# Nine feature-major tiles of a three-layer transformer computed as 512- and 256-column products in two PSUM banks each

## The chip, the cores and the metric

The kernel runs on one core of a Trainium2 chip. The metric is the time of one execution on the device in microseconds, the median over several runs. The core has TensorE (matrix products into PSUM, eight banks of 512 columns), VectorE, ScalarE and GpSimd (elementwise work), and SyncE, which issues the weight loads. Each has its own instruction stream, and they meet at semaphores only.

## The reference

Three layers work on 256 tokens of width 1024. The first two (a sparse-attention layer and a latent-attention layer, each with an MLP) are untouched here. The third is a hybrid layer:

```python
proj = h @ w_in            # q_m, k_m, v_m, gates, o, q_a, k_a, v_a, gate_pre
...
y_a = (jax.nn.sigmoid(o_pre.astype(f32)) * hm).astype(x.dtype)      # mLSTM branch
...
y_b = jnp.sum(wts[..., None] * jnp.stack(outs, axis=0), axis=0)     # dilated attention on q_a, k_a, v_a
...
g_a, g_b = jnp.split(jax.nn.sigmoid(gate_pre), 2, axis=-1)
merged = g_a * (y_a @ w_proj_a) + g_b * (y_b @ w_proj_b)
x = x + merged @ w_out
hf = rmsnorm(x, norm_ffn_g)
x = x + (jax.nn.silu(hf @ w_gate) * (hf @ w_up)) @ w_down
```

All is float32. `k_a` has 1536 columns, six tiles of 256; `y_a @ w_proj_a` has 1024, four tiles.

## The kernel before, in words

Every float32 weight and activation is kept as two parts, a high part rounded to the type that TensorE takes and the low remainder. A product W x is the sum of three: high x high, high x low, low x high (`three`, L628 to L630).

The weights come in chunks of 1 MB (2048 values in each of 128 partitions). Each goes through the same steps. SyncE loads it into one of two landing buffers (`raw`) once the chunk that was there has its low part. ScalarE copies it to `whi`, rounded (the **split**, `split_one`, L1769), once TensorE is through with the chunk that used this one of three split buffers. VectorE subtracts (`low_part`, L2417) and so makes `wlo`, the **low part**, and that frees the landing buffer; for a few chunks GpSimd does this (L1726). TensorE then uses the chunk. The order of each engine's work is written out by hand: `ahead(name)` and `split_to` on ScalarE, `low_ahead(name)` and `low_to` on VectorE say which chunks are prepared before a given step.

`feature_major(name, x, b)` makes one tile of 256 output features by 256 tokens. For each half of 128 features it adds up eight slices of the contraction, three products of 256 columns each, and both halves lie in one PSUM bank `b`. `open_bank` waits until the bank's last user has been read (`read`), `close_bank` signals `full`.

Around the change the third layer's TensorE program runs thus. Four mLSTM heads, each with one query tile qa0 to qa3 between its products; five key tiles ka1 to ka5 in banks 4 + (j + 2) % 4; four banks of transposes (`C.hT`); the value tiles va; the logits of the dilated attention; eight gate tiles g0 to g7 with the attention's products between them; the four projection tiles pa0 to pa3 in banks 2 and 3 by turns; pb0 and pb1 (`y_b @ w_proj_b`) in banks 4 to 7; then the output product co0 to co3, of which each waits for a tile `C.m{k}.lo` of the merged activations; then the FFN.

VectorE evacuates the tiles. `attention_copy` (L2982) multiplies a key tile by the norm's row scale (L2991); the loop at L3116 multiplies a projection tile by its gate (L3120); the loop at L3122 multiplies pb by its gate (L3128) and adds pa (L3129), and `merged_low` (L2590) makes the low part of each merged tile after ScalarE has made its high part. In the key stage VectorE also normalises the mLSTM's output, `hidden_normed` (L3027) and `hidden_gated` (L3030), between the key tiles. GpSimd has nothing to do in the third layer before the FFN.

The MLPs of the first two layers already have a form of 512- and 256-column products in their up step:

```python
for nt, k in tiles or ((nt, k) for nt in range(2) for k in range(KT)):
    nc.tensor.matmul(psum[:, 4 + 2 * j2 + nt, :], hi[:, k, nt * P:nt * P + P], xA[:, :, k, :],
                     start=k == 0, stop=False)
for nt in range(2):
    for k in range(KT):
        ins = nc.tensor.matmul(psum[:, 4 + 2 * j2 + nt, 0:SEQ], lo[:, k, nt * P:nt * P + P],
                               xA[:, 0, k, :], start=False, stop=k == KT - 1)
```

These are L842 and L846 of the profile: one product of the high weights with both parts of the activations side by side (512 columns), and one of the low weights with the high part (256 columns).

## Time and profile before

| | |
|---|---|
| median of 3 runs | 1105.75 us (1105.38 to 1105.99) |
| the profiled execution's own time | 1105.73 us |
| its span, first to last instruction | 1103.6 us |
| TensorE matmul / VectorE / ScalarE / GpSimd busy | 1090.9 / 757.8 / 600.3 / 149.6 us |
| mean granted TensorE clock | 0.999 of full |
| DMA | 194.00 MB, 176 GB/s in the mean |

The span leaves out 2.1 us at the two ends of the execution. Busy time is the union of an engine's records. TensorE's records overlap, since its products are pipelined: what a product costs is the distance from its start to the next start, not its recorded length.

### The profile page before, as it was taken

How to read it: one execution, taken by the hardware profiler on the slowest of the kernel's cores; microseconds unless marked ns; L12 is line 12 of the kernel's file. 1: busy time of each engine (PE TensorE's matmuls, PEld its weight loads, DVE VectorE, ACT ScalarE, POOL GpSimd, SP SyncE). 2: the span in 40 equal slices, each digit the busy share in tenths (PEclk: the TensorE clock that was granted, in tenths of full speed). 3: DMA queues.
4: the chain of work that ended last, by engine and by line, in shares of the span. 5: the costliest groups of instructions: out<-in, count | busy, mean ns of one | idle time of the engine just before them, and what ended most of it. 6: DMA issues, size and time to landing. Idle time of an engine off the chain costs nothing.

```text
span 1103.6 us, 17798 instructions
## 1 busy us (share of the span) xinstructions
PE 1090.9 (99%) x6977; PEld 973.0 (88%) x6977; DVE 757.8 (69%) x1054; ACT 600.3 (54%) x788; POOL 149.6 (14%) x113
## 2 busy tenths in 40 slices
PE   8999999999999999999999999999999999999997
PEld 7868888888998888888889999898899989999997
DVE  6774665656668466656557878576587577988884
ACT  6574644444698464444455546555555357546454
POOL 4652000000377220000030000000000002000003
PEclk9999999999999999999999999999999999999999
DMA  9836565556433156565645654446653556545631
GB/s 303 289 117 123 188 223 191 191 190 233 138 106 129 33 161 217 187 195 189 200 154 191 191 158 144 131 153 231 201 166 121 168 214 229 200 176 196 226 136 39
DMA packets 138929, 194.00 MB, mean 176 GB/s; under 512 B 7163, under 2 KB 113112, under 8 KB 138860
## 3 DMA queue, kind: packets, MB, share of 16 engines
q1 hardware_dynamic: 129004, 184.02, 50.7%
q10 hardware_dynamic: 9248, 8.95, 3.2%
q8 instruction: 47, 0.77, 0.3%
q0 software_dynamic: 608, 0.08, 0.1%
q14 instruction: 22, 0.18, 0.0%
HBM read 191.90 MB, written 6.37 MB: 180 GB/s over the span
## 4 chain that ended last, share of the span: by engine, by line
PE 91%; ACT 4%; DVE 4%; issue 1%; DVEq 0%; ACTq 0%
PE psum L628 22%; PE psum L629 22%; PE psum L630 22%; PE psum L842 11%; PE psum L846 6%; ACT arena L1755 3%; PE psum L716 2%; PE psum L746 1%; PE psum L1392 1%; PE psum L1419 1%; DVE arena L2711 1%; DVE st L2710 1%; PE psum L1353 0%; PE psum L904 0%; PE psum L906 0%
## 5 line engine op out<-in xcount | busy, mean ns | idle before, releaser
L2417 DVE TENSOR_TENSOR wlo<-raw,whi 128x2048 fp32r<-128x2048 f32 (+1 forms) x134 | 302.4, 2264 | 134.8 <-ACT whi L1769 133.7
L1769 ACT ACTIVATE whi<-raw 128x2048 fp32r<-128x2048 f32 (+1 forms) x149 | 277.4, 1871 | 174.0 <-PE psum L630 126.3
L628 PE MATMUL psum<-xA,whi 128*128 128x256 f32 x840 | 239.2, 285 | 0.0
L630 PE MATMUL psum<-xA,wlo 128*128 128x256 f32 x840 | 237.6, 283 | 0.0
L629 PE MATMUL psum<-xA,whi 128*128 128x256 f32 x840 | 237.6, 283 | 0.0
L1726 POOL TENSOR_TENSOR wlo<-raw,whi 128x288 fp32r<-128x288 f32 (+3 forms) x43 | 81.8, 1930 | 746.5 <-ACT whi L1769 746.2
L628 PEld LDWEIGHTS psum<-xA,whi 128*128 128x128 f32 x840 | 160.3, 191 | 2.9 <-DVE wlo L2648 0.9
L629 PEld LDWEIGHTS psum<-xA,whi 128*128 128x128 f32 x840 | 160.4, 191 | 1.1
L630 PEld LDWEIGHTS psum<-xA,wlo 128*128 128x128 f32 x840 | 160.3, 191 | 0.1
L842 PE MATMUL psum<-xA,whi 128*128 128x512 f32 x512 | 122.5, 390 | 0.0
L628 PE MATMUL psum<-whi,xC 128*128 128x512 f32 (+1 forms) x296 | 114.5, 387 | 0.0
L629 PE MATMUL psum<-wlo,xC 128*128 128x512 f32 (+1 forms) x296 | 114.2, 386 | 0.0
L630 PE MATMUL psum<-whi,xC 128*128 128x512 f32 (+1 forms) x296 | 113.9, 385 | 0.0
L842 PEld LDWEIGHTS psum<-xA,whi 128*128 128x128 f32 x512 | 95.5, 188 | 20.7 <-DVE xA L2525 1.3
L628 PE MATMUL psum<-whi,xA 128*128 128x512 f32 (+1 forms) x256 | 99.9, 390 | 0.0
L630 PE MATMUL psum<-whi,xA 128*128 128x512 f32 (+1 forms) x256 | 98.3, 384 | 0.0
L629 PE MATMUL psum<-wlo,xA 128*128 128x512 f32 (+1 forms) x256 | 98.2, 384 | 0.0
L1890 ACT ACTIVATE arena<-psum 128x512 f32<-128x512 f32 x32 | 19.1, 597 | 96.1 <-PE psum L846 96.0
L846 PEld LDWEIGHTS psum<-xA,wlo 128*128 128x128 f32 x512 | 65.6, 191 | 2.5
L846 PE MATMUL psum<-xA,wlo 128*128 128x256 f32 x512 | 66.4, 283 | 0.0
L630 PEld LDWEIGHTS psum<-whi,xC 128*128 128x128 f32 x296 | 55.6, 188 | 10.8
L628 PEld LDWEIGHTS psum<-whi,xC 128*128 128x128 f32 x296 | 55.7, 188 | 9.8
(311 smaller groups left out, 1685.7 us busy)
## 6 DMA issues: line engine op xcount, KB each, us to landing
raw<-in_w_in SPq DMA_DIRECT2D x42, 1024.0 KB, 5.0
raw<-in_mlp_w_up SPq DMA_DIRECT2D x32, 1024.0 KB, 5.3
raw<-in_mlp_w_down SPq DMA_DIRECT2D x32, 1024.0 KB, 4.8
raw<-in_w_gate SPq DMA_DIRECT2D x11, 1024.0 KB, 5.2
raw<-in_w_up SPq DMA_DIRECT2D x11, 1024.0 KB, 6.4
down_raw<-in_w_down SPq DMA_DIRECT2D x6, 1024.0 KB, 8.1
arena<-in_w_down SPq DMA_DIRECT2D x5, 1024.0 KB, 8.3
raw<-in_b_w_o SPq DMA_DIRECT2D x4, 1024.0 KB, 5.0
```

The source lines that it names most:

```text
L628: nc.tensor.matmul(out, lh, rh, start=start, stop=False, skip_group_check=skip)
L629: nc.tensor.matmul(out, lh, rl, start=False, stop=False, skip_group_check=skip)
L630: return nc.tensor.matmul(out, ll, rh, start=False, stop=stop, skip_group_check=skip)
L716: ins = nc.tensor.transpose(out[0:m, n * P:n * P + P], src, ident[:, :])
L746: ins = nc.tensor.transpose(out[:, (2 * i + blk) * P:(2 * i + blk) * P + P], hres[:, blk, k * P:k * P + P], ident[:, :])
L842: nc.tensor.matmul(psum[:, 4 + 2 * j2 + nt, :], hi[:, k, nt * P:nt * P + P], xA[:, :, k, :], start=k == 0, stop=False)
L846: ins = nc.tensor.matmul(psum[:, 4 + 2 * j2 + nt, 0:SEQ], lo[:, k, nt * P:nt * P + P], xA[:, 0, k, :], start=False, stop=k == KT - 1)
L1726: ins = T(wlo[split_of[c]][:, at:at + step], raw_bufs[raw_of[c]][:, at:at + step], f(whi[split_of[c]][:, at:at + step]), ALU.subtract)
L1755: ins = nc.scalar.activation(out, in_, func, **kw)
L1769: nc.scalar.activation(whi[split_of[c]][:, 0:n], raw_bufs[raw_of[c]][:, 0:n], ACT.Copy).then_inc(hi_sem, 1)
L1890: nc.scalar.activation(half_buf[:, j2, :].rearrange("p (a b) -> p a b", b=SEQ), psum[:, 4 + 2 * j2:6 + 2 * j2, SEQ:512], ACT.Copy).then_in ...
L2417: V.tensor_tensor(wlo[split_of[c]][:, 0:n], raw_bufs[raw_of[c]][:, 0:n], f(whi[split_of[c]][:, 0:n]), ALU.subtract).then_inc(lo_sem["dve"], 1)
```

## The change

Nine tiles, ka1 to ka5 and pa0 to pa3, are made by a new function `both_parts`. For each half of 128 features it takes a bank of its own. Eight products of the high weights with both parts of the activations write 512 columns, 0 to 255 high x high and 256 to 511 high x low; eight products of the low weights with the high part add 256 columns to the first half. The key tiles use banks 6 and 7, then 4 and 5, by turns; the projection tiles 2 and 3, 4 and 5, 6 and 7, 2 and 3. The two halves of each bank must then be added. ScalarE copies columns 256 to 511 of both banks to the result's place (`half_copy`), VectorE adds columns 0 to 255 (`parts_added`, two instructions of 256, which free the banks), and GpSimd multiplies by the row scale or the gate (`scale_tiles`). TensorE waits for GpSimd before the logits, VectorE before adding pa in the merge.

```diff
+            def both_parts(name, x, b):
+
+                c = index[name]
+                hi, lo = slot(c, KT, 256)
+                weights(c)
+                for nt in range(2):
+                    out = open_bank(f"{name}.{nt}", b + nt)
+                    for k in range(KT):
+                        nc.tensor.matmul(out, hi[:, k, nt * P:nt * P + P], x[:, :, k, :], start=k == 0, stop=False)
+                    for k in range(KT):
+                        ins = nc.tensor.matmul(out[:, 0:SEQ], lo[:, k, nt * P:nt * P + P], x[:, 0, k, :],
+                                               start=False, stop=k == KT - 1)
+                    close_bank(ins, f"{name}.{nt}")
+                chunk_done[c] = full[f"{name}.1"]
...
             for j in range(1, 6):
-                feature_major(f"ka{j}", xA, 4 + (j + 2) % 4)
+                both_parts(f"ka{j}", xA, (4, 6)[j % 2])
...
             for j in range(6):
                 wait_read(f"qa{j}.0")
-                wait_read(f"ka{j}.0")
+                pe.wait_ge(*(done[f"C.ka{j}"] if j else read["ka0.0"]))
...
             for j in range(4):
-                feature_major(f"pa{j}", xB, 2 + j % 2)
+                both_parts(f"pa{j}", xB, (2, 4, 6, 2)[j])
...
+            def scale_tiles():
+
+                pool.wait_ge(*read["C.rs"])
+                for name in tile_order:
+                    j = int(name[2])
+                    for nt in range(2):
+                        pool.wait_ge(*read[f"{name}.{nt}"])
+                    v = C[name[0:2]][:, 2 * j:2 * j + 2, :]
+                    run(T(v, v, row_scale.unsqueeze(1).to_broadcast([P, 2, SEQ]), ALU.mult), done[f"C.{name}"])
+                for j in range(4):
+                    pool.wait_ge(*done[f"C.gate{j // 2}"])
+                    for nt in range(2):
+                        pool.wait_ge(*read[f"pa{j}.{nt}"])
+                    v = C["pa"][:, 2 * j:2 * j + 2, :]
+                    run(T(v, v, C["gate"][:, 2 * j:2 * j + 2, :], ALU.mult), done[f"C.pa{j}"])
+
             for c in range(NC):
+                if chunks[c]["name"] == "ffn.g0":
+                    scale_tiles()
...
+            def half_copy(name, out):
+                for nt in range(2):
+                    act.wait_ge(*full[f"{name}.{nt}"])
+                b = bank[f"{name}.0"]
+                run(out, psum[:, b:b + 2, SEQ:512], ACT.Copy, done[f"C.{name}.half"])
...
             for j in range(1, 6):
                 ahead(f"ka{j}")
+                tile_half(f"ka{j}")
...
             split_to("pa2")
             out_high_c(3)
+            half_copy("pa0", C["pa"][:, 0:2, :])
             split_to("pb1")
+            for j in range(1, 4):
+                half_copy(f"pa{j}", C["pa"][:, 2 * j:2 * j + 2, :])
             ahead("pb1")
...
+            def parts_added(name, out):
+                dve.wait_ge(*done[f"C.{name}.half"])
+                for nt in range(2):
+                    run(V.tensor_tensor(out[:, nt, :], psum[:, bank[f"{name}.{nt}"], 0:SEQ], out[:, nt, :], ALU.add),
+                        read[f"{name}.{nt}"])
...
                 low_ahead(name)
+                j = int(name[2])
+                if name in tile_order:
+                    parts_added(name, C["ka"][:, 2 * j:2 * j + 2, :])
+                    return
...
                 low_ahead(f"pa{j}")
-                dve.wait_ge(*done[f"C.gate{j // 2}"])
-                dve.wait_ge(*full[f"pa{j}.0"])
-                run(V.tensor_tensor(C["pa"][:, 2 * j:2 * j + 2, :].rearrange("p a b -> p (a b)"), bk(f"pa{j}.0", 0, 512),
-                                    gate[:, 512 * j:512 * j + 512], ALU.mult), read[f"pa{j}.0"])
+                parts_added(f"pa{j}", C["pa"][:, 2 * j:2 * j + 2, :])
...
                 run(V.tensor_tensor(m, bk(name, 0, 512), gate[:, 2048 + 512 * k:2560 + 512 * k], ALU.mult), read[name])
+                dve.wait_ge(*done[f"C.pa{k}"])
                 run(V.tensor_tensor(m, m, C["pa"][:, 2 * k:2 * k + 2, :].rearrange("p a b -> p (a b)"), ALU.add),
```

How the instructions stand on three engines follows from this. On TensorE, the changed kernel from the second half of ka1 to the start of ka3 (L665 wide, L667 narrow products); before, these are 24 rows of L628, L629 and L630 in turn for each half, and a bank is waited for once a tile:

```order
L665 MATMUL psum<-xA,whi 128x512 [waits bank7_read]
L665 MATMUL psum<-xA,whi 128x512 x7
L667 MATMUL psum<-xA,wlo 128x256 x8
L665 MATMUL psum<-xA,whi 128x512 [waits bank4_read,weight_low_ready_dve]
L665 MATMUL psum<-xA,whi 128x512 x7
L667 MATMUL psum<-xA,wlo 128x256 x8
L665 MATMUL psum<-xA,whi 128x512 [waits bank5_read]
L665 MATMUL psum<-xA,whi 128x512 x7
L667 MATMUL psum<-xA,wlo 128x256 x8
L665 MATMUL psum<-xA,whi 128x512 [waits bank6_read,weight_low_ready_dve]
```

ka1 has banks 6 and 7, ka2 banks 4 and 5, and the last row, the first product of ka3, waits for the read of bank 6, two tiles after ka1 took it.

On ScalarE, before, from pa2's split (its first row) to the merged tiles; `whi<-raw` are the splits of pa2, then pa3, pb0, pb1, co0 and co1:

```order
L1769 ACTIVATE whi<-raw 128x2048 [waits bank1_full,weights_landed0,merge_gate_ready]
L1755 ACTIVATE xC<-arena 128x256 [waits bank0_read]
L1769 ACTIVATE whi<-raw 128x2048 [waits bank2_full,weights_landed1,activation_high_ready]
L1769 ACTIVATE whi<-raw 128x2048 [waits bank3_full,weights_landed0]
L1769 ACTIVATE whi<-raw 128x2048 [waits bank2_full,weights_landed1]
L1769 ACTIVATE whi<-raw 128x2048 [waits bank3_full,weights_landed0]
L1769 ACTIVATE whi<-raw 128x2048 [waits bank5_full,weights_landed1]
L1755 ACTIVATE xA<-arena 128x512 [waits merged_ready]
L1755 ACTIVATE xA<-arena 128x512 [waits merged_ready,activation_high_ready] x3
```

The same place in the changed kernel (L1806 is the split, `arena<-psum` the half copies):

```order
L1806 ACTIVATE whi<-raw 128x2048 [waits bank1_full,weights_landed0,merge_gate_ready]
L1792 ACTIVATE xC<-arena 128x256 [waits bank0_read]
L1792 ACTIVATE arena<-psum 128x512 [waits bank3_full,bank2_full,activation_high_ready]
L1806 ACTIVATE whi<-raw 128x2048 [waits bank3_full,weights_landed1,dilated_tile_half]
L1806 ACTIVATE whi<-raw 128x2048 [waits bank5_full,weights_landed0]
L1806 ACTIVATE whi<-raw 128x2048 [waits bank7_full,weights_landed1]
L1792 ACTIVATE arena<-psum 128x512 [waits bank5_full,bank4_full]
L1792 ACTIVATE arena<-psum 128x512 [waits bank7_full,bank6_full,dilated_tile_half]
L1792 ACTIVATE arena<-psum 128x512 [waits bank3_full,bank2_full,dilated_tile_half]
L1806 ACTIVATE whi<-raw 128x2048 [waits bank3_full,weights_landed0,dilated_tile_half]
L1806 ACTIVATE whi<-raw 128x2048 [waits bank5_full,weights_landed1]
L1792 ACTIVATE xA<-arena 128x512 [waits merged_ready]
```

The copy of pa0's half stands ahead of the splits of pa3, pb0 and pb1; those of pa1, pa2 and pa3 stand behind the split of pb1.

On VectorE, before, from pa0 to the first merged tile; L2417 is the low part of pa3, pb0, pb1, co0 in this order:

```order
L3120 TENSOR_TENSOR arena<-psum,arena 128x512 [waits bank2_full,merge_gate_ready,dilated_out_low]
L2417 TENSOR_TENSOR wlo<-raw,whi 128x2048 [waits weight_high_ready,bank2_read]
L3120 TENSOR_TENSOR arena<-psum,arena 128x512 [waits bank3_full,merge_gate_ready]
L2417 TENSOR_TENSOR wlo<-raw,whi 128x2048 [waits weight_high_ready,bank3_read]
L3120 TENSOR_TENSOR arena<-psum,arena 128x512 [waits bank2_full,merge_gate_ready]
L2417 TENSOR_TENSOR wlo<-raw,whi 128x2048 [waits weight_high_ready,bank2_read]
L3120 TENSOR_TENSOR arena<-psum,arena 128x512 [waits bank3_full,merge_gate_ready]
L2417 TENSOR_TENSOR wlo<-raw,whi 128x2048 [waits weight_high_ready,bank3_read]
L3128 TENSOR_TENSOR arena<-psum,arena 128x512 [waits bank4_full,merge_gate_ready]
L3129 TENSOR_TENSOR arena<-arena 128x512 [waits bank4_read]
L3128 TENSOR_TENSOR arena<-psum,arena 128x512 [waits bank5_full,merge_gate_ready,merged_ready]
```

And in the changed kernel (L3035 the adds, L2467 the low parts of pa3, pb0, pb1, co0):

```order
L3035 TENSOR_TENSOR arena<-psum,arena 128x256 [waits dilated_tile_half,dilated_out_low]
L3035 TENSOR_TENSOR arena<-psum,arena 128x256 [waits bank2_read]
L2467 TENSOR_TENSOR wlo<-raw,whi 128x2048 [waits weight_high_ready,bank3_read]
L3035 TENSOR_TENSOR arena<-psum,arena 128x256 [waits dilated_tile_half]
L3035 TENSOR_TENSOR arena<-psum,arena 128x256 [waits bank4_read]
L2467 TENSOR_TENSOR wlo<-raw,whi 128x2048 [waits weight_high_ready,bank5_read]
L3035 TENSOR_TENSOR arena<-psum,arena 128x256 [waits dilated_tile_half]
L3035 TENSOR_TENSOR arena<-psum,arena 128x256 [waits bank6_read]
L2467 TENSOR_TENSOR wlo<-raw,whi 128x2048 [waits weight_high_ready,bank7_read]
L3035 TENSOR_TENSOR arena<-psum,arena 128x256 [waits dilated_tile_half]
L3035 TENSOR_TENSOR arena<-psum,arena 128x256 [waits bank2_read]
L2467 TENSOR_TENSOR wlo<-raw,whi 128x2048 [waits weight_high_ready,bank3_read]
```

Each pair of adds now waits for ScalarE's half (`dilated_tile_half`), and the low part of the next chunk but one stands behind it, that of pb0 behind the adds of pa1.

## Rows read from the trace of the kernel before

**Rows 1.** The page, busy time of each engine, its share of the span, instructions.
```profile
PE 1090.9 (99%) x6977; PEld 973.0 (88%) x6977; DVE 757.8 (69%) x1054; ACT 600.3 (54%) x788; POOL 149.6 (14%) x113
```

**Rows 2.** Busy time by stretch, ka1 to ka5 (start:end length, engines, granted clock, DMA share, GB/s).
```profile
721.16:750.14 28.98, 28.98 (x242) 28.95 (x241) 22.50 (x30) 14.02 (x16) 0.00 (x0) 1.00 0.48 150
```

**Rows 3.** TensorE's timeline at the start of ka1 (start us, length us, instruction).
```profile
721.16 0.47 PE L628 MATMUL psum<-xA,whi 128*128 128x256 f32 x1
721.47 0.28 PE L629 MATMUL psum<-xA,whi 128*128 128x256 f32 x1
721.59 0.28 PE L630 MATMUL psum<-xA,wlo 128*128 128x256 f32 x1
```

**Rows 4.** TensorE's timeline, an up step of the second layer's MLP and what follows.
```profile
554.13 3.79 PE L842 MATMUL psum<-xA,whi 128*128 128x512 f32 x16
557.76 2.08 PE L846 MATMUL psum<-xA,wlo 128*128 128x256 f32 x16
559.67 0.40 PE L628 MATMUL psum<-whi,xC 128*128 128x512 f32 x1
```

**Rows 5.** VectorE's timeline in the key tiles.
```profile
733.64 0.69 DVE L2991 TENSOR_TENSOR arena<-psum,scales 128x512 f32<-128x512 f32 x1
734.37 1.76 DVE L3027 TENSOR_SCALAR arena<-arena,st 128x256 f32<-128x256 f32 x4
...
740.35 2.29 DVE L2417 TENSOR_TENSOR wlo<-raw,whi 128x2048 fp32r<-128x2048 f32 x1
```

**Rows 6.** ScalarE's timeline in the key tiles, two splits.
```profile
730.98 1.92 ACT L1769 ACTIVATE whi<-raw 128x2048 fp32r<-128x2048 f32 x1
...
747.60 1.92 ACT L1769 ACTIVATE whi<-raw 128x2048 fp32r<-128x2048 f32 x1 [1.74 <-DMA raw<-in_w_in]
```

**Rows 7.** ScalarE, a copy of 512 columns from PSUM.
```profile
760.30 0.69 ACT L1755 ACTIVATE arena<-psum,st 128x512 f32<-128x512 f32 x1 [0.71 <-PE psum L630]
```

**Rows 8.** VectorE, a 256-column product of PSUM and SBUF, and the instruction after it.
```profile
844.68 0.42 DVE L3083 TENSOR_TENSOR arena<-psum,arena 128x256 f32<-128x256 f32 x1
845.14 2.29 DVE L2417 TENSOR_TENSOR wlo<-raw,whi 128x2048 fp32r<-128x2048 f32 x1
```

**Rows 9.** TensorE, the first products of pb0 and of co0.
```profile
881.30 0.28 PE L628 MATMUL psum<-xC,whi 128*128 128x256 f32 x1
...
892.82 0.40 PE L628 MATMUL psum<-whi,xA 128*128 128x512 f32 x1
```

**Rows 10.** ScalarE's timeline, the splits of pb1 and co1.
```profile
875.80 1.92 ACT L1769 ACTIVATE whi<-raw 128x2048 fp32r<-128x2048 f32 x1 [3.84 <-PE psum L630]
...
887.32 1.92 ACT L1769 ACTIVATE whi<-raw 128x2048 fp32r<-128x2048 f32 x1 [3.84 <-PE psum L630]
```

**Rows 11.** VectorE, co0's low part, m0 begun, m0's low part, co2's low part.
```profile
883.58 2.29 DVE L2417 TENSOR_TENSOR wlo<-raw,whi 128x2048 fp32r<-128x2048 f32 x1 [1.32 <-ACT whi L1769]
885.78 0.69 DVE L3128 TENSOR_TENSOR arena<-psum,arena 128x512 f32<-128x512 f32 x1
...
889.85 0.69 DVE L2590 TENSOR_TENSOR xA<-arena,xA 128x512 fp32r<-128x512 f32 x1 [1.08 <-ACT xA L1755]
...
899.16 2.29 DVE L2417 TENSOR_TENSOR wlo<-raw,whi 128x2048 fp32r<-128x2048 f32 x1 [1.26 <-ACT whi L1769]
```

**Rows 12.** GpSimd, the low parts of ffn.g0 and ffn.u0, and a 512-element sum.
```profile
908.64 9.21 POOL L1726 TENSOR_TENSOR wlo<-raw,whi 128x2048 fp32r<-128x2048 f32 x2 [335.01 <-ACT whi L1769]
...
1083.36 1.28 POOL L1736 TENSOR_TENSOR hres<-hres,raw 128x512 f32<-128x512 f32 x1 [165.51 <-ACT raw L1755]
```

**Rows 13.** GpSimd's two stretches of L1688, then VectorE in the first of them.
```profile
312.44 3.21 POOL L1688 TENSOR_TENSOR arena<-arena 128x384 f32<-128x384 f32 x2 [3.72 <-ACT arena L1755]
...
327.69 1.72 POOL L1688 TENSOR_TENSOR arena<-arena 128x384 f32<-128x384 f32 x2
...
313.98 0.79 DVE L2845 TENSOR_TENSOR st<-st 128x2 f32<-128x2 f32 x1
314.80 0.17 DVE L2846 TENSOR_SCALAR st<-st 128x2 f32<-128x2 f32 x1
```

More of the change, by code:

```diff
@@ L433, in program @@
         plan("v_ones_written", ["C.ones"])
+        tile_order = [f"ka{j}" for j in range(1, 6)]
+        plan("dilated_tile_half", [f"C.{n}.half" for n in tile_order + [f"pa{j}" for j in range(4)]])
+        plan("dilated_tile_scaled", [f"C.{n}" for n in tile_order])
+        plan("projected_gated", [f"C.pa{j}" for j in range(4)])
         plan("output_gate_ready", ["C.so"])
@@ L2239, in _, with tile_half @@
             ahead("ka0")
+            def half_copy(name, out):
[3 more added lines that the diff above has]
+                run(out, psum[:, b:b + 2, SEQ:512], ACT.Copy, done[f"C.{name}.half"])
+            def tile_half(name):
+                half_copy(name, C[name[0:2]][:, 2 * int(name[2]):2 * int(name[2]) + 2, :])
             def mlstm(h):
@@ L2981, in _ @@
             run(V.tensor_copy(neg_row[:, SEQ:SEQ + P], neg_row[:, P:SEQ]), done["C.nm"])
+            def parts_added(name, out):
[3 more added lines that the diff above has]
+                        read[f"{name}.{nt}"])
             def attention_copy(name):
                 low_ahead(name)
+                j = int(name[2])
+                if name in tile_order:
+                    parts_added(name, C["ka"][:, 2 * j:2 * j + 2, :])
+                    return
                 dve.wait_ge(*full[f"{name}.0"])
-                j = int(name[2])
                 src = bk(f"{name}.0", 0, 512).rearrange("p (a b) -> p a b", b=SEQ)
```

## The prediction

> **What bounds the kernel now.** I read the page's engine shares first, then busy time by stretch, then the timelines of the stretches that the change touches. TensorE is busy 99% of the span, VectorE 69%, ScalarE 54%, GpSimd 14% [rows 1]. Over the five key tiles ka1 to ka5 TensorE is busy for all of 28.98 us, at a granted clock of 1.00, the 2.4 GHz level, and GpSimd does nothing [rows 2]. So TensorE sets the end, and work on the other engines costs nothing as long as TensorE doesn't wait for it. The change must be judged by two things: the TensorE time it removes, and the waits it makes.
>
> **The TensorE time removed.** A product of 256 columns starts 0.12 us after the one before it [rows 3]. The record's 0.28 us is its length in the pipeline, not its cost. An old tile is 48 such products: 48 x 0.12 = 5.76 us (five of them with 0.19 for the first make the 28.98 of rows 2). The new tile is 16 products of 512 columns and 16 of 256. The MLP's up step is that very work: 3.63 us from the first wide to the first narrow product, 1.91 us for the narrow ones, 5.54 us in all [rows 4]. Twice the columns cost 1.9 times as much, so only 0.22 us a tile is saved, and for nine tiles **-1.98 us**. That is a ceiling: 0.18% of 1105.73.
>
> **First wait: bank 6 before ka3.** The four rotating banks become two pairs (ka1 in 6 and 7, ka2 in 4 and 5, ka3 in 6 and 7 again). Before, ka3 took bank 5, long free; now it waits until VectorE has read ka1. VectorE gets to ka1 late, because it has the low part of ka3's weights and the norm of the first two heads in front: it starts ka1 at 733.64 [rows 5]. ScalarE's half of ka1 is no obstacle: ScalarE is free at 730.98 [rows 6] and a copy of 512 columns from PSUM takes 0.69 us [rows 7]. The add that frees bank 6 has 256 columns and takes 0.42 us (0.46 to the next) [rows 8]. With 0.1 us for the signal, ka3 starts at 733.64 + 0.42 + 0.1 = 734.16. TensorE would be ready at 721.16 + 0.19 + 2 x 5.54 = 732.43 [rows 3]. Wait: **+1.73 us**. Bank 7 is asked for half a tile later and is free by then. Between ka3 and ka5 nothing else is late: ka4 would start at 739.7 and its bank is read near 739.0 (behind two adds of 0.46, the second norm of 1.76 [rows 5] and a low part of 2.2); the margin is 0.7.
>
> **Second wait: weights of pb0.** In the projection stage the adds sit between the low parts on VectorE, and ScalarE copies pa1's half only after it has split pa3, pb0 and pb1 (the order rows above show both). The split of pb1 needs the weight buffer that pa2 frees. Before, pa2 ends at 881.30 - 5.76 = 875.54 [rows 9] and that split begins at 875.80, 0.26 us later [rows 10]. Take T as the end of pa2. The low part of pb0 is then ready at T + 0.26 + 1.92 (split [rows 10]) + 0.69 (half of pa1) + 0.05 + 2 x 0.46 (adds of pa1) + 2.29 (low part, [rows 11]) + 0.1 = T + 6.23. TensorE has pa3 to do and is ready at T + 5.54. Wait: **+0.69 us**. Before, this low part was made at 872 to 874 and only waited for its turn.
>
> **Third wait: the merged tile before co0.** The landing buffer of co0 is freed by the low part of pb0, so its load starts late too. Call L the end of that low part. From a low part's end to the split of the chunk that reuses its buffer takes 742.64 to 747.60 = 4.96 us [rows 5, 6]. Then 1.92 for the split, 0.07 to VectorE, 2.2 for the low part of co0 (883.58 to 885.78), four passes of 0.72 for m0 and m1, and 0.69 for m0's low part, which stands behind m1 [rows 11], and 0.1: L + 12.82. TensorE starts pb0 at L + 0.1 and needs 11.52 for pb0 and pb1 (881.30 to 892.82 [rows 9]): ready at L + 11.62. Wait: **+1.20 us**. Before, m0's low part was ready at 890.54 against 892.82, a cover of 2.3 us, and this is what the change uses up.
>
> **What is hidden.** Five plus four GpSimd products of 512 elements take about 1.28 us each [rows 12]; logits come 25 us after the last key tile, and pa0 to pa3 are wanted only in the merge, so their results are in time. ScalarE's nine copies (0.69 each) replace nothing but stand before splits that wait for a transfer anyway. On VectorE a read of 0.72 becomes two of 0.46. SyncE's loads are issued on the same releases; only those after pb0 move. Past co0 the low part of co2 (899.16 before, [rows 11]) ends near 905.1 and is wanted near 905.3, a margin of some 0.2 that I count as kept; GpSimd's low part for the first FFN chunk (908.64, 4.6 us a piece [rows 12]) comes near 917.0 against 917.1.
>
> **The sum.** -1.98 + 1.73 + 0.69 + 1.20 = +1.64 us on the profiled execution's 1105.73, which lies 0.02 below the median of the three runs: **1107.4 us**. The unseen prices are the signals between engines (0.1 taken, 0.04 to 0.3 the nearest rows: VectorE to its next instruction and TensorE to ScalarE) and TensorE's restart after a wait, bounded by nothing and the 0.19 of rows 3. For three waits that is -0.2 to +1.2 us. A change within 0.2%, which is 2.2 us, can't be told from none.
>
> **A rule against this change.** Rows first: GpSimd and VectorE hold each other up when both work from SBUF. Two GpSimd products take 3.21 us while VectorE makes a low part, and 1.72 without; in the same place a VectorE tensor_tensor of two elements takes 0.79 us where its neighbour takes 0.17 [rows 13]. So one side waits for the other's whole instruction. The Trainium skill (SBUF — State Buffer, section "SBUF: two separate sides") says the same: the pair of ports is an exclusive lock, taken against GpSimd by a VectorE instruction with two SBUF inputs, and whoever starts first keeps it. This trace agrees by the numbers of rows 13. Here the low parts are such instructions, the adds (one input in PSUM) are not.
>
> **The rivals.**
> 1. *GpSimd gets between the adds and the low part of pb0.* Its product for pa1 is released by the same add behind which that low part stands. If it gets the ports first, pb0 waits 1.28 us more, and the third wait follows it unchanged: 1107.4 + 1.28 = 1108.7. If it also catches one low part more that TensorE waits for, 1110.0. For it: the two are released within 0.1 us. Against it: VectorE restarts 0.04 us after its own instruction (rows 8: 844.68 + 0.42 to 845.14), before another engine has heard of it. It decides from the point at which the GpSimd product starts before the low part. Slower than before by 0.25% or more. Chance 0.22.
> 2. *The chains are looser than I count* (the load behind co0 lands sooner, or one wait vanishes into another engine's slack): one of the second and third waits is absent, 1105.5 to 1106.7. For it: 0.69 and 1.20 are small differences of long sums. Chance 0.15.
> 3. *No wait at all*, the change gives what its products save: 1105.73 - 1.98 = 1103.8. Against it: bank 6 is read by an instruction that stands in the trace at 733.64, 1.2 us after TensorE wants it. Chance 0.05, and even this is only on the edge of what can be told from no change.
> 4. *The margins past co0 break* (co2's weights, the first FFN chunk): each broken margin costs what it is late by, 0.3 to 1.5 us, 1107.7 to 1109. Chance 0.05, the rest of the forecast's upper side.
>
> **How the numbers follow.** The forecast has 0.53; its own range is 1107.2 to 1108.6, and about a quarter of it lies above 1107.96, the bound for slower. Slower: 0.13 + 0.22 + 0.02 = 0.37. Faster needs less than 1103.5, below the whole saving, so 0.04 for something I haven't seen. The rest, 0.59, is the same. The range from 1104.9 to 1110.0 takes in the rivals 1 and 2 and leaves out the third and any pile of broken margins.
>
> **What would show it.** In the new trace: wide and narrow products 0.227 and 0.12 us apart, 5.54 us a tile; TensorE idle about 1.7 us before ka3, ended by VectorE's add; about 0.7 before pb0, ended by a low part; about 1.2 before co0, ended by m0's low part; GpSimd's pieces for pa1 starting after pb0's low part. The forecast is wrong if TensorE doesn't stop before ka3, if a new tile takes other than 5.5 us, or if the low part of pb0 is longer than 2.3 us because GpSimd holds the ports.

## The result, and the profile after

The changed kernel takes **1114.95 us** (median of 4 runs, 1113.79 to 1116.28) against 1105.87 us for the kernel before (median of 4, 1105.38 to 1107.28): ratio 1.008, 95% interval 1.0062 to 1.0098. It is slower, by more than the whole range of the prediction (1104.9 to 1110.0). The profiled execution took 1113.8 us, its span is 1112.0 against 1103.6. (Some executions of every kernel here, of the one before too, are some 2 us longer, in the traces that have it by 3.4 us at the half clock about 10 us after the start; the medians take in both kinds, the stage lengths compared below contain none of it.)

The page of the changed kernel, busy time of each engine, and the chain that ended last. The second row is the first row of the page's part 4:

```profile
PE 1092.8 (98%) x6833; PEld 967.5 (87%) x6833; DVE 762.7 (69%) x1063; ACT 605.6 (54%) x797; POOL 167.2 (15%) x122
...
PE 82%; DVE 7%; ACT 6%; issue 3%; DMA 2%; ACTq 0%; DVEq 0%
```

TensorE has 144 instructions fewer and is busy 1.9 us longer than in [rows 1], although each new tile is shorter. Two things can do that at once: waits that lengthen the span, and a lower clock. Busy time by stretch, changed kernel, shows both (start:end length, then TensorE, its weight loads, VectorE, ScalarE, GpSimd, granted clock, DMA share, GB/s):

```profile
721.16:724.69 3.53, 0.26 (x2) 0.03 (x1) 3.00 (x3) 2.19 (x2) 0.00 (x0) 1.00 0.00 0
724.69:729.13 4.44, 4.44 (x17) 3.73 (x17) 1.50 (x9) 2.35 (x9) 0.00 (x0) 0.62 0.71 236
729.13:754.27 25.14, 25.14 (x146) 22.12 (x145) 23.55 (x24) 11.54 (x10) 7.19 (x4) 1.00 0.50 168
862.28:885.32 23.04, 22.63 (x131) 19.73 (x129) 11.61 (x11) 9.51 (x9) 3.71 (x2) 1.00 0.31 108
885.32:899.25 13.93, 11.74 (x97) 11.57 (x97) 9.50 (x12) 5.40 (x5) 5.40 (x3) 0.99 0.61 210
899.25:921.28 22.03, 22.03 (x91) 18.02 (x91) 17.00 (x16) 11.90 (x8) 4.14 (x1) 0.93 0.56 202
```

The same stages of the kernel before, for the last three rows:

```profile
858.16:881.30 23.14, 23.14 (x195) 23.14 (x194) 13.77 (x10) 7.52 (x5) 0.00 (x0) 1.00 0.48 154
881.30:892.82 11.52, 11.52 (x99) 11.52 (x98) 8.60 (x9) 4.99 (x4) 0.00 (x0) 1.00 0.50 180
892.82:913.25 20.43, 20.43 (x92) 16.84 (x91) 14.88 (x16) 12.01 (x8) 4.61 (x2) 1.00 0.59 207
```

The account of the span, from these rows and [rows 2]:

| stretch | before | changed | difference |
|---|---|---|---|
| start of ka1 | 721.16 | 724.69 | +3.53 |
| ka1 to ka5 (start to the transposes at 750.14 / 754.27) | 28.98 | 29.58 | +0.60 |
| from there to pa0 | 108.02 | 108.01 | -0.01 |
| pa0 to pb0 | 23.14 | 23.04 | -0.10 |
| pb0 to co0 | 11.52 | 13.93 | +2.41 |
| co0 to the last transposes | 20.43 | 22.03 | +1.60 |
| from there to the end | 190.35 | 190.72 | +0.37 |
| span | 1103.6 | 1112.0 | +8.40 |

**The start of ka1.** TensorE's timeline, changed kernel, against [rows 3]:

```profile
724.69 3.52 PE L665 MATMUL psum<-xA,whi 128*128 128x512 f32 x8 [3.27 <-DVE arena L3048]
728.01 1.28 PE L667 MATMUL psum<-xA,wlo 128*128 128x256 f32 x8
729.13 2.00 PE L665 MATMUL psum<-xA,whi 128*128 128x512 f32 x8
730.97 1.12 PE L667 MATMUL psum<-xA,wlo 128*128 128x256 f32 x8
731.92 2.00 PE L665 MATMUL psum<-xA,whi 128*128 128x512 f32 x8
```

TensorE stands before ka1, a place that the prediction doesn't name. What ends it is VectorE's L3048. VectorE's timeline, changed kernel, to be laid beside [rows 5]:

```profile
721.65 2.29 DVE L2467 TENSOR_TENSOR wlo<-raw,whi 128x2048 fp32r<-128x2048 f32 x1 [2.78 <-ACT whi L1806]
723.86 0.68 DVE L3048 SCALAR_TENSOR_TENSOR arena<-psum,scales 128x512 f32<-128x512 f32 x1
...
731.51 1.76 DVE L3086 TENSOR_SCALAR arena<-arena,st 128x256 f32<-128x256 f32 x4
733.30 0.88 DVE L3035 TENSOR_TENSOR arena<-psum,arena 128x256 f32<-128x256 f32 x2
734.22 2.61 DVE L3086 TENSOR_SCALAR arena<-arena,st 128x256 f32<-128x256 f32 x4
...
741.25 3.27 DVE L2467 TENSOR_TENSOR wlo<-raw,whi 128x2048 fp32r<-128x2048 f32 x1
```

L3048 reads qa3 out of its bank, behind a low part. qa3 stands in bank 4 + (3 + 3) % 4 = 6, and the pair rule puts ka1 in banks 6 and 7. The kernel before put ka1 in bank 7 and came to bank 6 only with ka4. The row was there to be read in the kernel before; VectorE's timeline, before:

```profile
724.19 0.69 DVE L2989 SCALAR_TENSOR_TENSOR arena<-psum,scales 128x512 f32<-128x512 f32 x1
```

It ends at 724.88, 3.72 us after TensorE was ready (721.16). The second half of ka1, at full clock, takes 1.84 + 0.95 = 2.79 us (729.13 to 731.92 above); the first half takes 4.44, at a granted clock of 0.62 in the mean. A first half at full clock is 2.98 us (all_mended, below), 0.19 of it the first product's, as in [rows 3]. So the stand costs 3.5 us itself and 4.44 - 2.98 = **1.46 us** more after it. Five tiles at 2 x 2.79 = 5.58 us, with those 0.19, are the 28.13 of all_mended and save 0.85 on 28.98. No wait shows before ka3: VectorE adds ka1 at 733.30 to 734.18, and ka3, now late itself, is due after it.

**The projection stage.** TensorE's timeline, changed kernel, the first products of pb0 and co0, against [rows 9]:

```profile
885.32 0.36 PE L632 MATMUL psum<-xC,whi 128*128 128x256 f32 x1 [0.41 <-DVE wlo L2467]
...
899.25 0.77 PE L632 MATMUL psum<-whi,xA 128*128 128x512 f32 x1 [2.19 <-DVE xA L2640]
```

VectorE and then ScalarE there, changed kernel, against [rows 11] and [rows 10]:

```profile
882.77 2.29 DVE L2467 TENSOR_TENSOR wlo<-raw,whi 128x2048 fp32r<-128x2048 f32 x1
...
893.30 2.29 DVE L2467 TENSOR_TENSOR wlo<-raw,whi 128x2048 fp32r<-128x2048 f32 x1 [4.16 <-ACT whi L1806]
...
898.41 0.69 DVE L2640 TENSOR_TENSOR xA<-arena,xA 128x512 fp32r<-128x512 f32 x1
```

```profile
879.42 1.92 ACT L1806 ACTIVATE whi<-raw 128x2048 fp32r<-128x2048 f32 x1 [3.67 <-PE psum L667]
881.24 1.21 ACT L1792 ACTIVATE arena<-psum 128x512 f32<-128x512 f32 x2
...
891.28 1.92 ACT L1806 ACTIVATE whi<-raw 128x2048 fp32r<-128x2048 f32 x1 [5.66 <-DMA raw<-in_w_out]
```

Both chains of the prediction are there, with their releasers. The low part of pb0 is late: 23.04 us for the stage, where the kernels below without that wait have 22.47, so the wait is 0.57. From the end of that low part (882.77 + 2.29 = 885.06) to co0's split it is 6.22 us, not the 4.96 of the prediction, and co0 starts 2.41 us late. After that the clock falls again: 22.03 us for 20.43, **1.60 us**.

### The profile page after: what moved, and what is told of

It is laid out like the page before. It is cut to its first block, busy times and chain, and to the rows that moved or that the text cites. A ratio compares the mean times of both kernels' runs of the same rounds, so it can differ in the third digit from the quotient of the medians.

```text
span 1112.0 us, 17562 instructions
## 1 busy us (share of the span) xinstructions
PE 1092.8 (98%) x6833; PEld 967.5 (87%) x6833; DVE 762.7 (69%) x1063; ACT 605.6 (54%) x797; POOL 167.2 (15%) x122
## 4 chain that ended last, share of the span: by engine, by line
PE 82%; DVE 7%; ACT 6%; issue 3%; DMA 2%; ACTq 0%; DVEq 0%
PE psum L632 18%; PE psum L633 18%; PE psum L634 18%; PE psum L861 11%; PE psum L865 6%; ACT arena L1792 4%; PE psum L665 3%; PE psum L735 2%; ACT whi L1806 1%; PE psum L667 1%; DVE wlo L2467 1%; PE psum L765 1%; PE psum L1411 1%; PE psum L1438 1%; DVE arena L2761 1%
## 5 line engine op out<-in xcount | busy, mean ns | idle before, releaser
L2467 DVE TENSOR_TENSOR wlo<-raw,whi 128x2048 fp32r<-128x2048 f32 (+1 forms) x134 | 305.1, 2284 | 135.4 <-ACT whi L1806 134.3
L1806 ACT ACTIVATE whi<-raw 128x2048 fp32r<-128x2048 f32 (+1 forms) x149 | 277.4, 1871 | 156.9 <-PE psum L634 106.2
L632 PE MATMUL psum<-xA,whi 128*128 128x256 f32 (+1 forms) x760 | 216.4, 285 | 0.0
L634 PE MATMUL psum<-xA,wlo 128*128 128x256 f32 (+1 forms) x760 | 214.9, 283 | 0.0
L633 PE MATMUL psum<-xA,whi 128*128 128x256 f32 (+1 forms) x760 | 214.9, 283 | 0.0
L632 PEld LDWEIGHTS psum<-xA,whi 128*128 128x128 f32 (+1 forms) x760 | 145.0, 191 | 2.8 <-DVE wlo L2698 0.9
L633 PEld LDWEIGHTS psum<-xA,whi 128*128 128x128 f32 (+1 forms) x760 | 145.0, 191 | 1.1
L634 PEld LDWEIGHTS psum<-xA,wlo 128*128 128x128 f32 (+1 forms) x760 | 145.0, 191 | 0.1
L861 PEld LDWEIGHTS psum<-xA,whi 128*128 128x128 f32 x512 | 95.5, 188 | 20.7 <-DVE xA L2575 1.3
L865 PEld LDWEIGHTS psum<-xA,wlo 128*128 128x128 f32 x512 | 65.6, 191 | 2.5
L865 PE MATMUL psum<-xA,wlo 128*128 128x256 f32 x512 | 66.4, 283 | 0.0
```

What stands on the lines that cost most here:

```text
L632: nc.tensor.matmul(out, lh, rh, start=start, stop=False, skip_group_check=skip)
L633: nc.tensor.matmul(out, lh, rl, start=False, stop=False, skip_group_check=skip)
L634: return nc.tensor.matmul(out, ll, rh, start=False, stop=stop, skip_group_check=skip)
L1806: nc.scalar.activation(whi[split_of[c]][:, 0:n], raw_bufs[raw_of[c]][:, 0:n], ACT.Copy).then_inc(hi_sem, 1)
L2467: V.tensor_tensor(wlo[split_of[c]][:, 0:n], raw_bufs[raw_of[c]][:, 0:n], f(whi[split_of[c]][:, 0:n]), ALU.subtract).then_inc(lo_sem["dve"], 1)
```

## The experiments

All times are medians; the profiled execution of each serves for the stages. The stages of the kernels side by side (us; the column ka1 is the distance from the start of the last pair of products before it to its own first product, 0.24 without a wait):

| kernel | ka1 | ka1-ka5 | pa0-pb0 | pb0-co0 | co0-transposes | span |
|---|---|---|---|---|---|---|
| before | 0.24 | 28.98 | 23.14 | 11.52 | 20.43 | 1103.6 |
| changed | 3.87 | 29.58 | 23.04 | 13.93 | 22.03 | 1112.0 |
| one_bank | 4.02 | 30.36 | 23.13 | 11.52 | 20.44 | 1110.7 |
| keys_alone | 3.99 | 29.53 | 23.14 | 11.52 | 20.44 | 1108.1 |
| projections_alone | 0.25 | 28.98 | 23.03 | 12.53 | 20.54 | 1107.7 |
| three_pairs | 0.25 | 29.56 | 23.03 | 13.94 | 22.13 | 1109.0 |
| halves_between | 4.37 | 29.42 | 22.47 | 11.52 | 20.43 | 1108.1 |
| both_mended | 0.24 | 29.19 | 22.46 | 11.52 | 20.44 | 1103.9 |
| short_products | 0.24 | 28.67 | 22.47 | 11.52 | 20.43 | 1103.5 |
| all_mended | 0.25 | 28.13 | 22.47 | 11.52 | 20.43 | 1102.5 |
| swapped_pairs | 0.25 | 30.02 | 23.03 | 14.00 | 22.02 | 1110.6 |

**1. one_bank: the kernel before with ka1's bank alone moved.**

```diff
-                feature_major(f"ka{j}", xA, 4 + (j + 2) % 4)
+                feature_major(f"ka{j}", xA, 6 if j == 1 else 4 + (j + 2) % 4)
```

> The kernel before with nothing changed but ka1's bank, 6 in place of 7, so that TensorE must wait for VectorE's read of qa3 before ka1. Theory A (the wait for a just written bank, and the clock that falls after it): TensorE stands for 3.3 us before ka1, the granted clock is 0.50 for some 3.4 us after that and costs 1.6 us more, the kernel is 5 us slower, 1111. Theory B (the wide tiles' extra work on ScalarE, VectorE and GpSimd is what costs, TensorE's first wait would be made up later): under 1 us slower, 1106 to 1107.

1112.46 us, ratio 1.0053 (1.0036 to 1.0070). TensorE's timeline, one_bank, the last pair of products before ka1 and ka1's first:

```profile
722.87 0.60 PE L1365 MATMUL psum<-arena 128*128 128x257 f32 x2
726.89 0.36 PE L628 MATMUL psum<-xA,whi 128*128 128x256 f32 x1 [3.43 <-DVE arena L2989]
```

Not one new product, copy or addition, and TensorE stands for 4.02 - 0.24 = 3.78 us, with 1.38 us more for tiles of the old kind behind it. The span is 7.1 us longer; the other 1.95 was lost before this place (722.87 for 720.92) and isn't the bank's. The bank by itself makes the loss at ka1.

**2, 3. keys_alone and projections_alone: one half of the change each**, the other tiles made as before (`feature_major`, with their old reads).

> The five key tiles changed, the four projection tiles as before. Theory A: the key stage alone costs 3.6 (wait) + 1.65 (clock) - 1.05 (products) = +4.2 us, 1110, and nothing is lost in the projection stage. Theory B: the losses come from both stages working together (late buffers carried on), so one alone costs under 2 us.

> The four projection tiles changed, the key tiles as before. Theory A: -0.7 (products) + 0.6 (wait before pb0) + 2.4 (wait before co0) + 1.6 (clock) = +3.9 us, 1109.8, with TensorE idle about 2.2 us before co0 and a clock of 0.50 behind it. If the wait before co0 is 1.2 us as I first worked it out and the clock holds: +1.1, 1107.

keys_alone: 1110.54 us, ratio 1.0043 (1.0026 to 1.0060), the loss at ka1 and nothing after it. projections_alone: 1109.05 us, 1.0024 (1.0013 to 1.0035). The wait at pb0 is the same 0.56, but at co0 only 1.01 us, and the clock holds (20.54). In this kernel alone TensorE loses another 1.01 us in the FFN, where its L1508 waits for VectorE's L2590. ScalarE's split of co0 starts at 887.79, VectorE's low part of pb0 ended at 882.96: 4.83 us for the load, where the changed kernel has 6.22. So the larger wait at co0, and the fall of the clock behind it, hang on one load that lands sooner or later by 1.4 us. It landed late in three kernels of three (changed, three_pairs, swapped_pairs), at the same place.

The traces show what is different about the late ones. DMA rows of the 3.3 us from the issue of co0's load, first the changed kernel (885.0:888.3), then projections_alone (882.9:886.2); a queue row has packets, MB and share, a load's row ends with the us from issue to landing:

```profile
q8 instruction: 1, 0.02, 1.8%
raw<-in_w_out SPq DMA_DIRECT2D x1, 1024.0 KB, 6.1
```

```profile
raw<-in_w_out SPq DMA_DIRECT2D x1, 1024.0 KB, 4.7
```

In the changed kernel a packet of 16 KB of the kind "instruction" runs inside the load, from 2.58 to 3.53 us after its issue; three_pairs and swapped_pairs have one too, 2.89 and 2.65 us after it. In projections_alone the next such packet comes 7.53 us after the issue, when the load has landed. A load ends with 16 packets of 4 bytes: 15 of them are through 4.6 us after the issue in the changed kernel and the last at 5.7, while in projections_alone all 16 are through at 4.4. Over the twelve traces, between 700 and 1000 us, the eight 1 MB loads with no other weight load in flight at their issue and an instruction packet starting 1.5 to 3.5 us after it took 6.06 to 6.40 us to land; the 262 without one in them have a median of 4.94, and 93% of them are under 5.3. That such a packet holds up one part of the load fits all this. No run moved the packet alone, and why it falls there once the key tiles are changed isn't shown.

**4. three_pairs: the changed kernel with three pairs of banks for the key tiles.**

```diff
-                both_parts(f"ka{j}", xA, (4, 6)[j % 2])
+                both_parts(f"ka{j}", xA, (2, 4, 6)[j % 3])
```

> The changed kernel with the key tiles' banks in three pairs (4 and 5, 6 and 7, 2 and 3 by turns) so that none is asked for while it is still to be read. Theory A: no wait and no fallen clock in the key stage, 5.3 us less than the changed kernel, 1109.7 at a changed kernel of 1115, that is 3 us over the kernel before. Theory B (GpSimd's products and the split adds hold up VectorE, and that holds TensorE): the key stage keeps most of its loss, over 1113.

1112.03 us, ratio 1.0055 (1.0038 to 1.0072): the wait at ka1 and its clock loss are gone, but the span falls only by 3.0 us. A new wait stands before ka4, which neither the prediction nor the expectation has. TensorE, and then VectorE, three_pairs:

```profile
739.88 2.11 PE L665 MATMUL psum<-xA,whi 128*128 128x512 f32 x8 [1.18 <-DVE wlo L2467]
```

```profile
734.88 2.62 DVE L3086 TENSOR_SCALAR arena<-arena,st 128x256 f32<-128x256 f32 x4
737.53 2.29 DVE L2467 TENSOR_TENSOR wlo<-raw,whi 128x2048 fp32r<-128x2048 f32 x1
```

The norm of the second two heads stands before ka4's low part and takes 2.62 us where the same four instructions take 1.76 elsewhere; GpSimd's first product (1.43 us, from 735.01) runs beside it. The prediction gave this place a margin of 0.7 us (for ka4's bank, with a norm of 1.76) and had not looked at the low part behind it.

**5, 6. halves_between and both_mended: another order on ScalarE**, on the changed kernel and on three_pairs:

```diff
             half_copy("pa0", C["pa"][:, 0:2, :])
+            split_to("pa3")
+            half_copy("pa1", C["pa"][:, 2:4, :])
+            split_to("pb0")
+            half_copy("pa2", C["pa"][:, 4:6, :])
             split_to("pb1")
-            for j in range(1, 4):
-                half_copy(f"pa{j}", C["pa"][:, 2 * j:2 * j + 2, :])
+            half_copy("pa3", C["pa"][:, 6:8, :])
```

> The changed kernel with ScalarE's halves of pa1 and pa2 copied ahead of the splits of pb0 and pb1, nothing else. If the order on ScalarE makes the waits before pb0 and co0: VectorE's low part of pb0 is ready about 8 us sooner, both waits (0.57 and 2.41 us) and the fallen clock in co0 to co3 (1.6 us) are gone, 4.6 us less than the changed kernel's 1115, 1110.4. If the split adds or GpSimd hold it up instead: under 1 us of that.

> Three pairs of banks for the key tiles and the halves between the splits. The key stage keeps its wait of 1.2 to 1.4 us for ka4's low part, behind which VectorE's norm stands (as in the run with three pairs), less 1.05 for the products; the projection stage gains 0.7 and waits for nothing. Within 0.5 us of the kernel before: 1105.4 to 1106.2.

halves_between: 1109.78 us, ratio 1.0032 (1.0020 to 1.0043). both_mended: 1105.72 us, 0.9993 (0.9983 to 1.0002). With the copies of pa1 and pa2 made before the later splits, pa0 to pb0 takes 22.47 us, 0.67 less than before, and both later waits and the second fall of the clock are gone. That is what four new tiles save.

**7. short_products: both_mended with GpSimd multiplying one column of each tile.** It leaves out nearly all of the multiplications by the row scale and the gate in these nine tiles.

> The same as both_mended, but GpSimd multiplies one column of each tile in place of 512: eight ninths and more of its work and of its use of the ports is left out, all waits stay. If GpSimd's products hold VectorE up through the shared ports: the four norm pieces (2.62 us beside a product) take 1.76, the low parts of 3.27 take 2.29, the wait before ka4 shrinks from 1.2 to about 0.4 us, and the kernel is 0.8 us faster than both_mended. If they don't: the same times as there.

1105.91 us, ratio 0.9992 (0.9982 to 1.0001), no shorter than both_mended by the medians; its key stage is 0.52 us shorter, where I expected 0.8. Three rows of VectorE in both_mended, then the same three in short_products:

```profile
734.21 2.61 DVE L3089 TENSOR_SCALAR arena<-arena,st 128x256 f32<-128x256 f32 x4
736.86 2.29 DVE L2470 TENSOR_TENSOR wlo<-raw,whi 128x2048 fp32r<-128x2048 f32 x1
...
741.24 3.27 DVE L2470 TENSOR_TENSOR wlo<-raw,whi 128x2048 fp32r<-128x2048 f32 x1
```

```profile
734.83 1.76 DVE L3089 TENSOR_SCALAR arena<-arena,st 128x256 f32<-128x256 f32 x4
736.62 2.29 DVE L2470 TENSOR_TENSOR wlo<-raw,whi 128x2048 fp32r<-128x2048 f32 x1
...
741.00 2.29 DVE L2470 TENSOR_TENSOR wlo<-raw,whi 128x2048 fp32r<-128x2048 f32 x1
```

The norm falls from 2.61 to 1.76 and the low part from 3.27 to 2.29: GpSimd's products are what lengthened them. The wait before ka4 shrinks by 0.52 us (key tiles 28.67 for 29.19) but doesn't go, since the norm still stands in front of the low part. GpSimd is held up in turn. Its products in short_products and in both_mended:

```profile
734.96 0.33 POOL L1725 TENSOR_TENSOR arena<-arena,scales 128x1 f32<-128x1 f32 x1 [160.90 <-DVE arena L3038]
739.88 1.14 POOL L1725 TENSOR_TENSOR arena<-arena,scales 128x1 f32<-128x1 f32 x1 [4.59 <-DVE arena L3038]
...
749.14 0.19 POOL L1725 TENSOR_TENSOR arena<-arena,scales 128x1 f32<-128x1 f32 x1 [3.74 <-DVE arena L3038]
```

```profile
740.11 2.24 POOL L1725 TENSOR_TENSOR arena<-arena,scales 128x512 f32<-128x512 f32 x1 [4.34 <-DVE arena L3038]
...
750.82 1.28 POOL L1725 TENSOR_TENSOR arena<-arena,scales 128x512 f32<-128x512 f32 x1 [3.11 <-DVE arena L3038]
```

One column takes 0.19 us alone and 1.14 beside VectorE's product of 1024 (739.74 to 740.97); 512 elements take 1.28 alone and 2.24 in that place. GpSimd waits 0.95 and 0.96 us, whatever its own size; both times it started 0.14 or 0.13 us after VectorE's product of 1.2 us, so this is about what was left of that product.

**8. all_mended: both_mended with VectorE's low parts of ka4 and ka5 put before what they waited behind.**

```diff
             attention_copy("ka1")
+            low_to(index["ka4"])
             hidden_normed((2, 3))
             attention_copy("ka2")
+            low_to(index["ka5"])
```

> both_mended with the low parts of ka4 and ka5 moved on VectorE ahead of the second norm and of the first gating. If the wait before ka4 is VectorE's order alone: no wait left, products save 1.05 + 0.7, the kernel is 1.5 to 1.8 us faster than before, 1104.0. If another wait takes its place (gating or transposes late, the landing buffer freed too late for ka5): 1105 or more.

1104.32 us, ratio 0.9978 (0.9968 to 0.9988). Busy time by stretch, all_mended: TensorE is busy for all of each stage, at full clock:

```profile
721.64:749.77 28.13, 28.13 (x163) 24.74 (x162) 24.04 (x31) 15.83 (x20) 8.87 (x3) 1.00 0.45 150
857.85:880.32 22.47, 22.47 (x131) 19.76 (x129) 14.77 (x13) 9.33 (x8) 3.88 (x3) 1.00 0.47 157
```

TensorE's timeline, all_mended, the wide products of ka1's two halves, 2.98 us apart:

```profile
721.64 2.20 PE L665 MATMUL psum<-xA,whi 128*128 128x512 f32 x8
...
724.62 2.00 PE L665 MATMUL psum<-xA,whi 128*128 128x512 f32 x8
```

28.98 - 28.13 = 0.85 and 23.14 - 22.47 = 0.67: the nine tiles save 1.52 us, and the profiled span is 1.1 shorter than that of the kernel before (ka1 begins 0.48 later there, by work ahead of it that wasn't touched).

**9. swapped_pairs: the changed kernel with its two bank pairs exchanged**, so that the wait that was predicted before ka3 can show by itself:

```diff
-                both_parts(f"ka{j}", xA, (4, 6)[j % 2])
+                both_parts(f"ka{j}", xA, (6, 4)[j % 2])
...
-                    token_part(f"va{j}", part, ((4, 5), (6, 7))[j])
+                    token_part(f"va{j}", part, ((6, 7), (4, 5))[j])
```

> The changed kernel with the two bank pairs of the key tiles exchanged: ka1, ka3, ka5 in banks 4 and 5, ka2 and ka4 in 6 and 7 (and va0, va1 likewise). ka1 no longer needs the bank in which qa3 is still to be read, so it should start at about 721.3 without a wait, and now the wait of the prediction can show: ka3 is due at 721.3 + 2 x 5.58 = 732.5, VectorE's two additions of ka1 stand at 733.3 to 734.2 behind the norm, so TensorE should stand for about 1.7 us. Theory A (a stand of 1.7 us leaves the clock at full, as those of 1.0 and 1.2 us did): key stage 28.98 - 1.05 + 1.7 = 29.6 us, projection stage as in the changed kernel (+3.9 us against before: waits 0.57 and 2.41, clock 1.60, products -0.67), together 4.6 us above before. Theory B (a stand of 1.7 us lowers the clock to 0.50 as the 2.2 us ones did): 1.6 us more, 6.2 us above before. Theory C (my bank reading of ka3 was wrong and no wait is there): about 2.9 us above before.

1112.41 us, ratio 1.0047 (1.0033 to 1.0061). TensorE's timeline, swapped_pairs, then busy time in ka3's first half:

```profile
733.19 1.11 PE L667 MATMUL psum<-xA,wlo 128*128 128x256 f32 x8
735.77 1.40 PE L665 MATMUL psum<-xA,whi 128*128 128x512 f32 x5 [1.47 <-DVE arena L3035]
```

```profile
735.77:738.64 2.87, 2.87 (x16) 2.53 (x17) 2.73 (x5) 0.33 (x1) 1.43 (x1) 1.00 0.73 258
```

The wait is there: 735.77 - 733.19 = 2.58 us, 1.63 more than the 0.95 of narrow products without a wait. The clock stays at full behind it (theory A). The key tiles take 30.02 us, 0.4 over the 29.6 expected: the first half of ka1 (2.98) and three halves from ka3 on (2.87 to 2.90) are 0.08 to 0.19 us longer than 2.79, which the expectation leaves out.

**10. all_again: the same kernel as all_mended**, measured with the kernels of experiment 9.

> The version with all three mends once more, in five rounds, to narrow its interval: products -1.7 us and nothing lost to waits or to the clock, so a ratio of 0.998 to 0.999 with an interval wholly below 1. If the 1.3 us of the first measurement were the luck of which executions lost clock at the start, the interval would take in 1.

1104.63 us (1104.04 to 1106.38, 11 runs), ratio 0.9988 (0.9979 to 0.9997). The interval lies below 1 again, but overlaps the first only in part; 0.1 to 0.2% is what the mended version gains on the kernel before, and the 1.52 us of its stages are 0.14%. Its lead over the changed kernel is near 0.9% (spans 1112.0 and 1102.5).

## Why the prediction was wrong

- **The products: right in kind, 0.46 us less than said.** Forecast 9 x 0.22 = 1.98 us; measured, stage against stage without waits (all_mended), 0.85 in the key tiles and 0.67 in the projections, 1.52. A tile took 5.58 us, not 5.54 (1.84 + 0.95 a half). Here wide and narrow products change twice as often as in [rows 4], whose pieces are of 16; that this is the 0.04 is a guess.
- **"First wait: bank 6 before ka3": this step failed.** It asks who read bank 6 last for ka3 alone, and takes ka1's banks for free. They weren't: qa3, in the old rotation, still stood in bank 6. TensorE waited there for 3.5 us, and the 1.73 us foreseen at ka3 didn't show: ka3, itself later, found its bank read. The piece of TensorE's order that stands in the section on the change begins at ka1's second half; the row above it, with the wait for bank 6 of the first half, is the one that was needed. Experiment 1 shows that the bank alone makes the loss, experiment 9 that the wait before ka3 exists at nearly its size (1.63 for 1.73) once ka1's is taken away. With experiments 1 and 9 both mechanisms are shown.
- **What the prediction has no step for: the clock after a wait.** At two stands, of 3.5 and 2.4 us, the granted clock fell to half for 3.4 us, and they cost 1.46 and 1.60 us beyond themselves. That is 3.06 of the 8.4 us. The sum has nothing for it: the prediction gives "TensorE's restart after a wait" at most 0.19 us.
- **"Second wait: weights of pb0": right.** 0.57 for 0.69, ended by the low part that was named. The half copy took 0.60, not 0.69, the split 1.82 to the next instruction, not 1.92, and the two additions the 0.92 that were counted; the signal to TensorE took 0.26 (885.06 to 885.32), not 0.1.
- **"Third wait: the merged tile before co0": right in its chain, half in size.** 2.41 for 1.20. The term that was mis-sized is the load, 6.22 for 4.96 from low part to split; the others together are off by 0.05. In projections_alone, where the load took 4.83, the wait was 1.01. The late loads are those with an instruction packet inside (experiments 2 and 3).
- **"What is hidden": nearly right, with a cover too thin.** ka4 has no wait in the changed kernel only because ka1 was late. Take that away and its low part, which I hadn't placed, is late by 1.3 us (experiment 4). The margins past co0 held in the changed kernel but for the clock: the stage is 20.43 or 20.44 us again in every kernel whose clock held there, except projections_alone (20.54), which also lost 1.01 us in the FFN, within the 0.3 to 1.5 us of rival 4.
- **Rival 1, GpSimd getting in before pb0's low part, didn't happen.** The low part began at 882.77, GpSimd at 882.91, and the low part took its 2.29 us. The rule itself bites elsewhere. Rows first: experiment 7 takes GpSimd's elements away and VectorE's norm falls from 2.61 to 1.76. The Trainium skill (SBUF — State Buffer, section "SBUF: two separate sides") lets VectorE contend when it has two SBUF inputs or runs in a mode of two ports; its account agrees with the low part's 3.27 and GpSimd's 2.24. The norm has one tensor input from SBUF, with scalars of one column from SBUF beside it, and was held too; whether it ran in a mode of two ports isn't shown.
- **The direction** had a chance of 0.37 for slower. It came from the right kind of reason, waits at shared buffers and banks, but the largest was at a place that wasn't looked at.

The account closes: 3.53 (ka1) + 1.46 (clock) - 0.85 (products) + 0.57 - 0.67 (pb0, products) + 2.41 (co0) + 1.60 (clock) = 8.05 us at the last transposes, of 8.03 measured (921.28 - 913.25). The last 0.37 us lie behind TensorE's last product, where the twelve profiles differ by up to 0.8 us, and aren't explained.

## What to carry to other kernels

When tiles change banks, list for every tile the last reader of its bank, the first tile most of all, since it meets whatever the stage before left there; a time in the old trace (here 724.19 + 0.69 against 721.16) then gives the wait. A wait on TensorE of 2 us or more is to be priced twice, as itself and as the clock behind it (some 1.5 us here). Where a helper engine's work is put between two others, its place in their queues decides more than its length: a third pair of banks, two copies and two low parts moved took this kernel from 0.8% slower to 0.1 to 0.2% faster.

## What the hardware showed that I had not expected

Long and short stands differed in what the clock did. Recorded as idle before the first product: 3.27, 3.39, 3.43 and 3.77 us (ka1 in the changed kernel, keys_alone, one_bank, halves_between) and 2.19, 2.19 and 2.25 us (co0 in the changed kernel, three_pairs, swapped_pairs) all came with a granted clock at half, the 1.2 GHz level, for 3.4 us, which began between 0.4 us before that product and 1.2 us after it; after 1.47, 1.18, 0.79, 0.41 and 0.28 us it stayed at full. Busy time by stretch, three_pairs, the stage before and the one behind co0's stand:

```profile
882.18:896.12 13.94, 11.75 (x97) 11.58 (x97) 9.51 (x12) 5.41 (x5) 5.42 (x3) 1.00 0.63 207
896.12:918.25 22.13, 22.13 (x90) 18.06 (x91) 16.99 (x16) 11.88 (x8) 3.98 (x1) 0.92 0.58 203
```

The Trainium skill (TensorE: Matmul & The Clock Gate, section "What's actually happening") has an idle array fall to 1.2 GHz and come back after work; the traces agree (1.00 before the stand, 0.50 for 3.4 us, then 1.00). Measured against the same stretch at full clock, one fall cost 1.30 to 1.46 us at ka1 with products of 512 columns, 1.38 there in one_bank with products of 256, and 1.6 to 1.7 at co0. Nothing between 1.47 and 2.19 us was run, so where it turns, and whether the length of the stand alone decides, stays open.
